# Five projections of a second block as block products, with first taps on ScalarE and the convolutions' sums in PSUM

## The reference

```python
h = rmsnorm_2(x, norm1_g[l])
proj = h @ w_in[l]
qa, ka, va, qm, km, vm, om, gm, mg = split_cols(proj, IN_SPLITS)
ya = windowed_gqa(qa, ka, va, attn_q_gain[l], attn_k_gain[l], rel_bias_table, attn_sink[l])
ym = mlstm_branch(qm, km, vm, om, gm, ...)
gates = jax.nn.sigmoid(mg + merge_b[l])
u = gates[..., :D_MODEL] * (ya @ w_branch_attn[l]) + gates[..., D_MODEL:] * (ym @ w_branch_mlstm[l])
x = x + u @ w_out[l]
x = x + hier_moe(...)
```

## Time and profile before

| | |
|---|---|
| median of 3 runs | 1687.57 us (1685.78 to 1687.7) |
| the profiled execution | 1688.09 us, its span 1686.3 us |
| mean granted TensorE clock | 0.993 |
| PE busy | 1630.7 us, 97% of the span |
| DVE, ACT, POOL busy | 737.4, 387.8, 192.5 us |
| DMA | 303.63 MB, 180 GB/s on average |

### The profile page before, as it was taken

How to read it: one execution, slowest core, us unless ns; L and a number is a source line. 1 busy time by engine, 2 the same in 40 slices (tenths; PEclk the granted TensorE clock), 3 DMA queues, 4 the chain that set the end, 5 groups by cost and what they waited for, 6 DMA issues and landing times.

```text
span 1686.3 us, 18096 instructions
## 1 busy us (share of the span) xinstructions
PE 1630.7 (97%) x7006; PEld 947.7 (56%) x7006; DVE 737.4 (44%) x1526; ACT 387.8 (23%) x823; POOL 192.5 (11%) x206
## 2 busy tenths in 40 slices
PE   7999999999999999999999999999999999997986
PEld 4444454578888888875444678744633333333332
DVE  3387786455454535451677256325521121121211
ACT  4443663510000000022365224100511111111110
POOL 1000000000000000010000424115022222221221
PEclk9999999999999999999999999999999999999999
DMA  5531114030222222223111111636899999999996
GB/s 189 125 75 50 51 51 140 11 113 0 100 78 72 100 100 75 106 66 117 50 50 50 51 50 51 206 97 234 352 394 417 416 418 417 424 413 417 422 416 235
DMA packets 75138, 303.63 MB, mean 180 GB/s; under 512 B 13037, under 2 KB 14194, under 8 KB 62124
## 3 DMA queue, kind: packets, MB, share of 16 engines
q1 hardware_dynamic: 64432, 287.40, 43.3%
q0 software_dynamic: 9872, 12.91, 3.7%
q10 hardware_dynamic: 748, 2.15, 0.3%
HBM read 306.99 MB, written 15.73 MB: 191 GB/s over the span
## 4 chain that ended last, share of the span: by engine, by line
PE 87%; DMA 8%; DVE 2%; SPq 2%; issue 1%; ACT 0%; POOL 0%; POOLq 0%; DVEq 0%; ACTq 0%
PE ps L1216 11%; PE ps L1260 11%; PE ps L1665 11%; PE ps L1084 9%; PE ps L1357 7%; PE ps L1504 6%; PE ps L1682 5%; DMA W<-in_w_expert_up 5%; PE ps L1120 3%; PE ps L1080 3%; PE ps L1543 3%; PE ps L1569 3%; DMA W<-in_w_expert_down 2%; PE ps L1368 2%; PE ps L1139 1%; SPq L766 1%
## 5 line engine op out<-in xcount | busy, mean ns | idle before, releaser
L3017 DVE SCALAR_TENSOR_TENSOR smb<-smb,ptb,ps 64x512 f32<-64x512 f32 x34 | 38.2, 1124 | 273.9 <-ACT smb L2139 273.9
L1084 PE MATMUL ps<-W 128*128 128x512 f32 (+1 forms) x336 | 149.3, 596 | 1.9 <-DMA W<-in_w_in 1.9
L1665 PE MATMUL ps<-W,cmask 128*64 128x512 f32 x480 | 132.5, 609 | 4.6 <-DMA W<-in_w_expert_up 3.9
L1665 PE MATMUL ps<-W,gb 128*64 128x512 f32 x480 | 129.5, 599 | 2.8 <-DMA W<-in_w_expert_up 2.7
L1357 PE MATMUL ps<-W 128*128 128x512 f32 x272 | 122.3, 599 | 1.9 <-DVE yT L2657 1.9
L1216 PE MATMUL ps<-yT,W 128*128 128x256 f32 x512 | 113.0, 379 | 0.0
L1682 PE MATMUL ps<-W,ptb 128*64 128x512 f32 x464 | 106.0, 598 | 4.2 <-DVE ptb L3023 3.3
L1260 PE MATMUL ps<-W,mix 128*128 128x256 f32 x496 | 108.5, 379 | 0.0
L1216 PEld LDWEIGHTS ps<-yT,W 128*128 128x128 f32 x512 | 97.3, 190 | 13.2
L1084 PEld LDWEIGHTS ps<-W 128*128 128x128 f32 (+1 forms) x336 | 61.2, 188 | 75.3 <-issue 72.9
L1260 PEld LDWEIGHTS ps<-W,mix 128*128 128x128 f32 x496 | 94.3, 190 | 12.8
(11 more groups left out here) (479 smaller groups left out, 2433.4 us busy)
## 6 DMA issues: line engine op xcount, KB each, us to landing
W<-in_w_expert_up SPq DMA_DIRECT2D x25, 2048.0 KB, 34.8
W<-in_w_expert_down SPq DMA_DIRECT2D x24, 2048.0 KB, 33.4
W<-in_w_expert_gate SPq DMA_DIRECT2D x22, 2048.0 KB, 32.0
W<-in_w_in SPq DMA_DIRECT2D x16, 2048.0 KB, 7.7
W<-in_w_up SPq DMA_DIRECT2D x8, 2048.0 KB, 8.3
W<-in_w_down SPq DMA_DIRECT2D x8, 2048.0 KB, 7.7
W<-in_w_out SPq DMA_DIRECT2D x4, 2048.0 KB, 7.8
W<-in_w_expert_gate SPq DMA_DIRECT2D x8, 1024.0 KB, 21.8
```

The costliest lines, as they stand in the source:

```text
L1084: ins = pe.matmul(ps[0:n, bank, :], wv[:, k, j * P:j * P + n], hT[:, k, :], start=(k == 0), stop=(k == KT - 1))
L1665: ins = pe.matmul(ps[64 * part:64 * part + 64, 2, :], xsT[s][:, k, :], w[part][:, k, :], start=(k == 0), stop=(k == KT - 1))
```

## The change

It does the following.

- The five projections are made as block products: 35 side products (`side_product`), numbered together with the 28 of the merge gates (n = 0 to 62; seven each for `qm`, `km`, `qa`, `vm`, `om`, then the gates). The keys and the two `va2` groups stay dense. 25 products come before the windowed attention, ten stand in its steps (`beside`), one in every other step.
- POOL makes the sums of `hT` (`side_h_sum`) at the start of the second block and the weight sums of each chunk (`side_w_sums`) in three parts. The sums of `hT` lie where x was. So SP stores x to DRAM (`x_dram`, four DMAs of 512 KB) and loads it again after the last gate product.
- The running sum of each convolution lies in a PSUM bank (`CONV_BANK`). ACT writes the first tap there (`tap`), DVE adds four more, and ACT's silu reads it. All eight now come before the windowed attention.
- The queries' norms: per pair of query chunks, PE makes sums of squares with tokens on the partitions (`pair_sums`), ACT takes the root of 16 columns, DVE inverts them (`pair_recip`), PE spreads them over the heads' rows (`spread_roots`) and DVE multiplies (`query_norm`).
- The gate rows, scans and columns come before the windowed attention too, and the columns use bank 3.
- The order of chunks is changed, the last down chunk's slot is given free at its product P3, and two small inputs are counted among the others.

```diff
         chunks2 = [cols_of(w2, a, n) for a, n in
-                   ((VM, 512), (KVA2, 256), (QA2, 512), (QM, 512), (KM, 512), (OM, 512))]
+                   ((KVA2, 256), (QM, 512), (KM, 512), (QA2, 512), (VM, 512), (OM, 512))]
+        C_SIDE = C_P2 + 1
...
-            chunk_done[C_DOWN + q] = (down_prod, down_count(q, "P4" if q != 6 else "P3"))
+            chunk_done[C_DOWN + q] = (down_prod, down_count(q, "P4" if q < 6 else "P3"))
...
+        def side_bank(n):
+            if n < N_AHEAD:
+                return 4 + n % 4
+            return 4 + n % 2 if n < 35 else 5 if n < 49 else 4 + (n - 49) % 4
+
+        X_KEPT = [48 if i == 1 else 32 for i in range(NT)]
+        CONV_BANK = (2, 3, 2, 3, 2, 1, 2, 1)
+        CONV_AFTER = {4: 0, 6: 1, 8: 2, 10: 3, 12: 4, 14: 5, 16: 6, 18: 7}
...
+                if n == 1:
+                    sp.wait_ge(turn_src, 4 * NORM[T_N1] + NT)
+                    for i in range(NT):
+                        sp.dma_start(x_dram[i * P:(i + 1) * P, :], x[:, i, :]).then_inc(x_load[i], 16)
...
-                    sp.wait_ge(gate_read, 28)
+                    sp.wait_ge(side_read, 63)
+                    for i in range(NT):
+                        sp.wait_ge(x_load[i], X_KEPT[i])
+                        sp.dma_start(x[:, i, :], x_dram[i * P:(i + 1) * P, :]).then_inc(x_load[i], 16)
...
+            pool.wait_ge(turn_src, 4 * NORM[T_N1] + NT)
+            side_w_sums(0, 0)
+            pool.wait_ge(turn_evac, turned_by(T_N1, NT - 1))
+            side_h_sum(0, b12, b11)
+            side_h_sum(1, b22, side_h[0])
+            side_w_sums(0, 1)
+            side_h_sum(2, b22, b12)
+            side_w_sums(0, 2)
+            side_h_sum(3, side_h[1], b21)
+            for c in range(1, 5):
+                for part in range(3):
+                    side_w_sums(c, part)
...
+            side_product(0)
+            side_product(1)
+            turn(T_N1, [2])
+            dense(0)
+            turn(T_N1, [3])
+            pe.wait_ge(turn_evac, turned_by(T_N1, NT - 1))
+            dense(1)
+            dense(2)
+            side_product(2)
+            norm_sums(1)
+            for n in range(3, 7):
+                side_product(n)
+            gate_rows_out()
+            for n in range(7, 14):
+                side_product(n)
+            free_when[3] = (qk_ready, 4)
+            gate_columns()
+            for n in range(14, 23):
+                side_product(n)
+            free_when[2] = (qk_ready, 7)
+            pair_sums(0, 2)
+            side_product(23)
+            free_when[1] = (qk_ready, 8)
+            spread_roots(0, (0, 1))
+            side_product(24)
...
+            def tap(c):
+                if c >= 2:
+                    act.wait_ge(qk_ready, c - 1)
+                act.wait_ge(side_read, 7 * (c // 4) + SIDE_READ["P4" if c % 4 > 1 else "P3"])
+                act.activation(ps[:, CONV_BANK[c], :], convin[:, c, 0:512], ACT.Copy, scale=convw[:, c, 0:1]
+                               ).then_inc(first_tap, 1)
...
+            for n in range(7, 20):
+                side_keep(n)
+                if n in CONV_AFTER:
+                    tap(CONV_AFTER[n])
...
+                if n - 2 in CONV_AFTER:
+                    silu(CONV_AFTER[n - 2])
...
+            def conv(at):
+                dve.wait_ge(first_tap, at + 1)
+                acc = ps[:, CONV_BANK[at], :]
+                for w in range(1, CONV):
+                    ins = dve.scalar_tensor_tensor(out=acc, in0=convin[:, at, w:w + 512], scalar=convw[:, at, w:w + 1],
+                                                   in1=acc, op0=ALU.mult, op1=ALU.add)
...
+            for n in range(4, 20):
+                side_post(n)
+                if n in CONV_AFTER:
+                    conv(CONV_AFTER[n])
+                if n == 6:
+                    gate_scans()
+                if n == 13:
+                    gate_cols()
```

More of the change, by code:

```diff
@@ new lines, in pair_sums @@
+            def pair_sums(pair, bank):
+                pe.wait_ge(sq_done, 2 * pair + 3)
+                group(bank, hstd_done, pair + 2)
+                for q in range(2):
+                    for i in range(NT):
+                        ins = pe.matmul(ps[:, bank, 8 * q + 2 * i:8 * q + 2 * i + 2],
+                                        squares[:, q, i * P:(i + 1) * P], ones[:, 0:P:64],
+                                        start=True, stop=True)
+                ins.then_inc(ssb_done, 1)
@@ new lines, in spread_roots @@
+            def spread_roots(pair, banks):
+                pe.wait_ge(pair_roots, pair + 1)
+                for q, bank in enumerate(banks):
+                    group(bank, qkn_done, 2 * pair + q + 2)
+                    for i in range(NT):
+                        for h in range(2):
+                            at = 16 * pair + 8 * q + 2 * i + h
+                            ins = pe.matmul(ps[64 * h:64 * h + 64, bank, i * P:(i + 1) * P],
+                                            hrs[:, at:at + 1].broadcast_to([P, 64]), ident[:, :], start=True, stop=True)
+                    ins.then_inc(roots_spread, 1)
@@ L2001, in window_pairs @@
                         exps(a)
-                    for n in whole(a):
-                        dense(n)
+                    for n in beside(a):
+                        side_keep(n)
+                    if a == 0:
+                        pair_std(1, 7)
             window_pairs()
@@ L2711, in _ @@
             window_pairs()
+            for n in beside(len(PAIRS) + 2):
+                side_post(n)
             dve.wait_ge(em_ready, 1)
```

608 lines of the change are left out of this document (293 added, 315 removed).

## The result

The changed kernel takes **1697.31 us** (median of 4 runs, 1696.66 to 1699.75) beside 1686.93 for the kernel before (1685.78 to 1687.70) on the same chip: ratio 1.0065, 95% interval 1.0047 to 1.0082. Run once more beside the experiments it took 1698.69 beside 1687.78: 1.0062, 1.0049 to 1.0075. It is slower by 10 to 11 us. My forecast was 1688.5, my range ended at 1697.0, and the nearest of the rivals was B (1695.5).

What follows compares the result with a forecast made beforehand. TensorE was taken to bound the stretch before the recurrence, any shift there reaching the end whole. -16.5 + 3.1 + 2 + 11.5 + 0.8 = +0.9 us gave 1688.5 us; 8-in-10 range 1680 to 1697.

Steps and rivals of the forecast that it cites:

- B: Rival: GpSimd's sums hold VectorE in and before the window, +8 us, 1695.5; sign: stretch over 207 us; chance 0.30.
- Work alone: TensorE's projections, head sums, norms and vanished old waits: 16.5 us less before any new waits, the ceiling.
- Start: Start of the second block: TensorE waits 3.1 us for tile 3's rows, their evacuation and the sums of hT.
- tile 3's turn: At the start, tile 3's rows come from VectorE 1.7 us after TensorE is ready to turn them.
- Gate columns: Before the gate columns, TensorE waits for bank 3, freed by ScalarE's silu: 2 us (0 to 4.5).
- Window: Windowed attention: TensorE waits for VectorE's scaling now that only every other step has a product: 11.5 us (3 to 16).
- base of 70 us: TensorE's work in windowed attention without waits: turns, scores, values, ten products, pair sums and spreading, 70 us in all.
- the lock missing every time: Windowed attention if no GpSimd sum ever holds VectorE: waits of about 3 to 6 us.
- Bank 4: At the end of windowed attention, bank 4 needs product 34's reader: 0.8 us.
- The rest at nothing: After windowed attention: no change; a late second branch chunk, 1690 to 1692, had chance 0.04.
- A: Rival: the work is what counts, TensorE's queue is rarely held: -8 us, 1680; chance 0.30.
- C: Rival: the experts' weight stream swallows any shift, time stays 1687.6; counted within the forecast's chance of 0.36.

Runs made afterwards that it cites:

- e10: Changed kernel with the window's ten products halved, two GpSimd sums timed, gate columns behind product 14, x reloaded behind the second branch chunk: 1676.30 us.
- e3: Changed kernel with all twenty GpSimd weight sums of the five projections cut to 8 columns: 1685.07 us.
- e2: Changed kernel with only the four GpSimd weight sums in windowed attention cut to 8 columns: 1691.31 us.
- e11: Changed kernel with two added GpSimd waits, so two weight sums begin only after VectorE scaled pairs 3 and 4: 1692.60 us.
- e6: Changed kernel with product 27's eight matmuls run once more, in front of the turn that waits for VectorE: 1695.36 us.
- e8: Changed kernel with the convolutions' running sums in SBUF, not PSUM banks, first tap still on ScalarE: 1702.77 us.
- e12: Changed kernel with halved products, later gate columns and two timed GpSimd sums, but x reloaded ahead of the second branch chunk: 1679.51 us.

## Why the prediction was wrong, by its own steps

The step that failed is the price of the window. I had it wait for VectorE's scaling and priced these waits alone: 11.5 us, where the runs show 17. The waits were in fact shorter, 7.2 us. The rest came from terms that the sum had at nothing or too small: the lower clock behind the lock, small holds within the groups of scores, and the work itself. Two further terms had the same hole, the gate columns (2 us, measured 4.7) and the rest behind the stretch (nothing, measured up to 4.6).

*Work alone, -16.5.* Nearly right. In e10, with halves and with the clock up all the time, the stretch without its listed waits is 185.2 us; before, it was 197.4. That is -12.2 where my terms without the old waits make -13.8. Ahead of the window the work was 1.6 shorter than my terms, within it 2.8 longer. Products took 3.45 us each, a pair's sums 1.70 (1.6 expected), a pair's spreading 1.90 (2.05 expected).

*Start, 3.1.* Measured 1.43 + 0.27 + 1.29 = 3.0. The sum holds, but one of its parts stood elsewhere. The first product waits 1.43 for VectorE to copy out the turned rows of tile 1, which I had not seen. That makes TensorE later, and of my 1.7 at tile 3's turn it leaves 0.27. The total came out right because the same lateness is paid once, wherever it stands.

*Gate columns, 2 (0 to 4.5).* The wait came as forecast, 2.23 at ScalarE's silu, with 0.67 at the group before. The two groups behind it then took 8.70 us up to the next start in place of 6.91. Together that is 4.7; e3 beside e2 puts the whole at 4.8. I had the wait and missed the 1.8 of clock behind it.

*Window, 11.5 (3 to 16).* This is the term that failed. From the first scores at 862.14 to 950.08 it took 87.9 us; less the 70 of work and the 0.87 at the end, 17 in place of 11.5. The places were right: the lock at pair 3 (I had 4.3 for the turn of step 5, listed 1.44 + 1.98), 1.87 and 1.17 in the late steps. Added up, the waits in the window are 7.2 us, less than I had walked to. The excess is of three kinds. The clock behind the lock takes 3.2: 2.5 at product 27 and 0.7 at the scores before it, about half of the 6.8 us at the lower level. Small holds inside seven groups of scores take 4.1 (L1522 with 1.5 where 0.92 is usual, or 1.2 where 0.70 is); one of the seven is the group at 883.64, held 0.7 in e2 and e11, where the clock is up. With halves all but 0.45 of them are gone in e10. And my base of 70 us is 2.8 too small by e10: there the window takes 74.1 with one wait of 0.38 and the 0.87, the 0.45 of holds included. That makes 7.2 + 3.2 + 3.6 + 2.8 = 16.8. e6 shows the clock's part by itself: a stretch 3.7 us shorter than in the first profile (5.3 beside the second, which has two more falls). With the four sums cut, e2's window takes 8.7 over base and end, where I had 3 to 6 "with the lock missing every time".

*Bank 4, 0.8.* Measured 0.87.

*The rest at nothing.* Failed by 3.9 to 4.6 in the first profile, by 0.3 in the second; over the profiles with x ahead the wait was anything from none (e8) to 3.56 us. I had asked how long 8.4 MB take and written that at 0.3 MB/us they come 1 us too late, then gave it a chance of 0.04. They were issued behind the last gate product near 1090 and landed at 1119.1 (issue at 1097.88, 21.2 us): 29 us, the 0.29 MB/us that I had as the outer bound. The earlier trace rows had the rate of the experts' stretch, where transfers of 2 MB are queued; the trace of before had the rate of this place. There the same loads without x, 6.3 MB, were issued from 1083.40 and the last landed at 1105.0, 14.1 us after its issue at 1090.93: 21.6 us, 0.29 MB/us as well. Why it is lower here no run isolates; these loads are partly of 0.5 and 1 MB. And I had priced a wait of 1 us as 1 us, without the 1.8 of slow matmuls that can stand behind it.

*The rivals.* B is what happened, with 7.5 in the stretch (it said +8, the forecast +0.9, and "over 207" was its mark; measured 207.85). B's own point from which it decides, two sums meeting normalizations, was met twice over: all four did, and the window's 17 us are near B's 16. But B had these 16 as waits on the lock. TensorE's listed waits there are 7.2, and the other 10 are the clock, the holds and the work. So its size is right in part by luck. A's claim, that the work is what counts, fell. But its size was about right for a kernel with halves whose waits are cured: e10's stretch is 10.3 us shorter than before, and A had -8. C fell in every run: the last stretch takes 481.6 to 485.0 us whatever comes ahead.

The trace of before had the clock's term. Behind a wait of 2.75 us it shows ten matmuls of the recurrence (twenty records) in 3.49 us and a product in 4.30; the same in the changed kernel without a wait ahead take 2.44 and 3.62. It also had a wait of 1.95 us, in the window's steps at 918.39, behind which the clock stayed at 1.00, so it allowed a range and not one price:

```profile
987.05 3.49 PE L1416 MATMUL ps<-W 128*128 128x129 f32 x20 [2.75 <-DVE mix L2745]
990.33 4.30 PE L1504 MATMUL ps<-W 128*128 128x256 f32 x16
```

```profile
984.58 2.44 PE L1508 MATMUL ps<-W 128*128 128x129 f32 x20
...
987.29 3.62 PE L1432 MATMUL ps<-W 128*128 128x256 f32 x16
```

## What to carry to other kernels

A wait that you put into a TensorE-bound stretch is to be priced with the slow matmuls that can follow it; look in the trace for the groups behind waits that are already there and take their excess too, as the upper end of the term. When work is taken off TensorE and given to GpSimd and VectorE, ask of each GpSimd operation not how long it takes but which VectorE operation it meets; a wait on GpSimd itself, so that it works in a gap, cost nothing that the profile shows and gave 6 us here. Finer pieces of dense work between the steps of a latency-bound loop (halves at each step, not wholes at every other) are cover for both.

## What the runs showed of the hardware

- **The clock can fall behind a wait, and the fall cost from half the wait to as much again.** In the branch products four 512-column matmuls took 5.37 us in place of 3.60 behind waits of 2.68, 3.47, 3.55 and 3.56 us, and 3.67 behind waits of 0.57, 0.95, 1.58 and 1.81. The two waits at the lock, 1.44 and 1.98, were followed by 6.8 us at the lower level. It is not the wait alone: behind the same 1.61 us at the first expert the group took 3.65 us in the kernel before and in e8, e10 and e12, and 5.06 to 5.35 in the ten other profiles. A fall can also come with no wait just ahead of it: product 25 took 5.41 us in e6, e11 and the changed kernel's second profile. What went before in those runs differs by the waits further up; which of it decides, no run here isolates.
- **GpSimd holds VectorE's one-input operation too.** Two tensor_scalar on SBUF, 0.62 us together, waited out one sum each and took 4.77. An addition of two numbers per row, 0.16 us, took 2.25 beside a third. An operation with an input in PSUM was not held: the 32 taps of the convolution took 754 ns on average, none over 757, though 12 of them ran beside a sum, and 1060 on average in SBUF, with four over 2.7 us. The Trainium skill, "SBUF — State Buffer", section "Who interferes with whom", counts tensor_scalar among the operations that can take the port shared with GpSimd, and says that the one issued later is held for the whole instruction. The trace agrees.
- **The lock can come twice in a row.** GpSimd's second sum followed its first by 0.08 us. The first of VectorE's two scalings ended between them (TensorE's turn behind it began at 880.75, 0.2 us after the first sum's end), and the second was held again, by the second sum.
